# Finer orders at stage borders and in a mixer: weight splits, half-tile transposes, bank pairs, forget logits and last level scores

## The reference

```
x = layernorm(a*x + concat(retention(x@w_in), pool(x@w_in)) @ w_out)        # wout1, ln1
x = layernorm(a*x + (silu(conv3(gate)) * val) @ w_down)                    # up1, down1, ln2
x = x + 0.5*rms(swiglu(rms(x), ffn1_w_in, ffn1_w_down))                    # upA, downA
q_a,f_a,i_a,g_a,q_b,k_b,v_b,f_b,gates = rms(x) @ w_in_2                    # win2, 36 half blocks
o_a = rms(hgrn2(q_a,f_a,i_a)) * silu(g_a)   # scores with products of decays, in levels
o_b = softmax(q_b k_b^T + cumulated log sigmoid(f_b)) v_b                  # forgetting attention
x = x + rms((gate0*(o_a@w_a) + gate1*(o_b@w_b)) @ w_out_2)                 # brA, brB, wout2
x = x + rms(cross_attention(rms(x), rms(mem)) @ w_mo)                      # mq, mk, mv, mo
x = x + 0.5*rms(swiglu(rms(x), ffn2_w_in, ffn2_w_down))                    # upB, downB
```

## Time and profile before

| | us |
|---|---|
| median of 3 runs (1146.81 to 1151.43) | 1147.98 |
| profiled execution, device time | 1149.37 |
| its span | 1147.3 |
| PE busy | 1114.6 (97%) |
| PEld busy | 931.9 (81%) |
| DVE busy | 702.4 (61%) |
| ACT busy | 589.7 (51%) |
| DMA, mean over the span | 174 GB/s |

### The profile page before, as it was taken

The page is one execution under the profiler, slowest core; times in us unless marked ns, Lnnn a source line. Parts: engine busy times, 40 slices in busy tenths (PEclk is TensorE's granted clock), DMA queues, the critical chain, the costliest instruction groups (busy, mean ns, idle before and its releaser), DMA issues.

```text
span 1147.3 us, 13384 instructions
## 1 busy us (share of the span) xinstructions
PE 1114.6 (97%) x5370; PEld 931.9 (81%) x5370; DVE 702.4 (61%) x806; ACT 589.7 (51%) x777; POOL 41.7 (4%) x49
## 2 busy tenths in 40 slices
PE   7999999999999999999999999999999989999998
PEld 5887888888788888888888888888888767888886
DVE  4548566665776555566976765657547355765541
ACT  4463655554374634466545535536355456655441
POOL 1900000000000000000000000010000000000000
PEclk9999999999999999999999999999999999999999
DMA  9654655555575555475343443356555324656540
GB/s 370 212 182 143 216 177 172 183 181 185 176 244 183 184 183 183 147 257 172 123 147 116 142 147 127 130 211 230 177 177 202 124 74 146 197 182 195 183 162 37
DMA packets 125901, 200.14 MB, mean 174 GB/s; under 512 B 6288, under 2 KB 74048, under 8 KB 125712
## 3 DMA queue, kind: packets, MB, share of 16 engines
q1 hardware_dynamic: 122624, 187.78, 48.8%
q0 software_dynamic: 3216, 11.51, 2.8%
HBM read 198.22 MB, written 1.05 MB: 174 GB/s over the span
## 4 chain that ended last, share of the span: by engine, by line
PE 87%; DVE 7%; ACT 3%; issue 2%; DMA 1%; DVEq 0%; SPq 0%; ACTq 0%
PE ps L573 22%; PE ps L575 22%; PE ps L574 21%; PE ps L714 4%; PE ps L610 3%; PE ps L612 3%; PE ps L611 3%; PE ps L889 2%; DVE rest L1576 2%; ACT high L1101 1%; PE ps L1019 1%; PE ps L1032 1%; DVE rest L1581 0%; PE ps L675 0%; PE ps L677 0%
## 5 line engine op out<-in xcount | busy, mean ns | idle before, releaser
L1576 DVE TENSOR_TENSOR rest<-raw,high 128x2048 fp32r<-128x2048 f32 (+1 forms) x136 | 306.1, 2279 | 140.7 <-ACT high L1101 140.7
L573 PE MATMUL ps<-high,xt_high 128*128 128x512 f32 x896 | 356.5, 398 | 3.7 <-DVE rest L1576 2.1
L575 PE MATMUL ps<-high,xt_rest 128*128 128x512 f32 x896 | 350.6, 391 | 0.0
L574 PE MATMUL ps<-rest,xt_high 128*128 128x512 f32 x896 | 350.0, 391 | 0.0
L1101 ACT ACTIVATE high<-raw 128x2048 fp32r<-128x2048 f32 (+1 forms) x133 | 248.6, 1902 | 37.4 <-DMA raw<-in_ffn_w_down_dram 22.5
L573 PEld LDWEIGHTS ps<-high,xt_high 128*128 128x128 f32 x896 | 169.1, 189 | 37.4 <-issue 2.5
L575 PEld LDWEIGHTS ps<-high,xt_rest 128*128 128x128 f32 x896 | 168.9, 188 | 36.1
L574 PEld LDWEIGHTS ps<-rest,xt_high 128*128 128x128 f32 x896 | 169.2, 189 | 33.4
L1581 DVE SCALAR_TENSOR_TENSOR rest<-raw,wgain,high 128x512 fp32r<-128x512 f32 x176 | 119.0, 746 | 46.6 <-ACT high L1105 46.6
L1105 ACT ACTIVATE high<-raw,wgain 128x512 fp32r<-128x512 f32 x176 | 110.9, 721 | 9.5 <-DMA raw<-in_ffn_w_in_dram 9.5
L1323 ACT ACTIVATE act<-ps,recips 128x256 f32<-128x256 f32 x44 | 18.5, 471 | 98.6 <-PE ps L575 98.6
(11 more groups left out here) (320 smaller groups left out, 1313.9 us busy)
## 6 DMA issues: line engine op xcount, KB each, us to landing
raw<-in_w_in_dram SPq DMA_DIRECT2D x92, 512.0 KB, 4.2
raw<-in_ffn_w_in_dram SPq DMA_DIRECT2D x88, 512.0 KB, 4.7
raw<-in_w_up_dram SPq DMA_DIRECT2D x44, 512.0 KB, 4.6
raw<-in_ffn_w_down_dram SPq DMA_DIRECT2D x44, 512.0 KB, 4.1
raw<-in_w_down_dram SPq DMA_DIRECT2D x22, 512.0 KB, 4.3
raw<-in_w_out_dram SPq DMA_DIRECT2D x16, 512.0 KB, 4.5
raw<-in_w_mkv_dram SPq DMA_DIRECT2D x16, 512.0 KB, 4.6
raw<-in_w_branch_a_dram SPq DMA_DIRECT2D x8, 512.0 KB, 4.2
```

The lines of the kernel that those rows point to most:

```text
L573: pe.matmul(out, sh, wh, start=first, stop=False)
L574: pe.matmul(out, sh, wr, start=False, stop=False)
L575: mm = pe.matmul(out, sr, wh, start=False, stop=last)
L1576: vec.tensor_tensor(rest[:, slot, c], raw[:, slot, c], high[:, slot, c].bitcast(F32), ALU.subtract).then_inc(sem("lead_rest") if lead else ...
```

## The change

1. `wout1` begins with pair 1 instead of pair 0 (its weights are loaded in that order), and pair 0 comes next. For `mo` the new table gives the order that it had.
2. At the borders of `ln1` and `ln2`, DVE splits two units of the next stage before the statistics of tile 0 instead of three, and the third between the statistics of the two column halves.
3. At all four borders, transposes are ordered by column half. Only half 0 of tile 0 is transposed before the last products of tile 1, half 1 behind them; in `first_units` half 0 of tile 1 stands before unit 2 of tile 0, half 1 behind it.
4. `post_norm` on ACT puts the addition of the offset to the first partial sum (L1182) ahead of the second square instead of behind it.
5. In the mixer DVE does the subtraction of the forget logits at the head of u = 5 and the scan and memsets at the head of u = 7, each before that step's weight split.
6. The scores of level 128 are computed between the two halves of the half block u = 16 and 25, and only the outputs behind it.

```
+HALF_ORDER = {"wout1": ((1, 1), (0, 1), (0, 0), (1, 0)), "mo": ((0, 0), (1, 0), (0, 1), (1, 1))}
...
-                    for n, half in enumerate(HALVES[name]):
-                        for j in range(2):
-                            load_block((u + 2 * n + j,), w, j * NB, (half,))
+                    for n, (j, half) in enumerate(HALF_ORDER[name]):
+                        load_block((u + n,), w, j * NB, (half,))
...
-            def unit(u, products, wait=None):
+            def unit(u, products, between=None):
...
+                    if between and n == len(products) // 2:
+                        between()
...
-            def tile_transposes(key, src, ready, tt):
-                for q in range(2):
+            def tile_transposes(key, src, ready, tt, parts=(0, 1)):
+                for q in parts:
                     ready(tt, q)
                     transposes((key, 2 * tt + q), [src(tt, 4 * q + c) for c in range(4)])
...
+                    if n == 0:
+                        tile_transposes(key, src, ready, tt, (1,))
                     if n < 2:
                         wait_taken((key, 2 * tt + n))
                     elif tt == 0:
-                        tile_transposes(key, src, ready, 1)
+                        tile_transposes(key, src, ready, 1, (0,))
...
-            alternate("wout1", 0)
+            alternate("wout1", 1, 0)
...
-                    tile_transposes("x1", from_x, x1_ready, 0)
-
-            by_tiles(UNIT["wout1"] + 1, lambda tt: [(k, chunk_products("wout1", (1, 0, 1)[k], int(k > 0), tt),
+                    tile_transposes("x1", from_x, x1_ready, 0, (0,))
+
+            by_tiles(UNIT["wout1"] + 1, lambda tt: [(k, chunk_products("wout1", (0, 0, 1)[k], int(k > 0), tt),
...
-                if lv == 128:
-                    wait_taken(*(("lv", hf, v, g) for v in (0, *LEVELS, 128) for g in range(1 if v else 2)))
...
+            def level_outputs(hf):
+                wait_taken(*(("lv", hf, v, g) for v in (0, *LEVELS, 128) for g in range(1 if v else 2)))
...
+                last_levels = [n for n in HG_SLOT[u] if HG_STEPS[n][1] == 128]
                 if u >= LEAD:
-                    half_block("win2", j, half)
+                    half_block("win2", j, half, between=(lambda: levels(last_levels[0])) if last_levels else None)
...
                 square_half(tt, 0, name)
                 if between:
                     split_to(between)
+                act.wait_ge(sem("squared"), squared[0])
+                part_offset(tt)
                 square_half(tt, 1, name)
-                act.wait_ge(sem("squared"), squared[0] - 1)
-                part_offset(tt)
                 settle()
...
                 for n in range(2):
+                    if n == 1 and between:
+                        split_to(between)
...
-            split_to(UNIT["up1"] + LEAD)
-            layer_stats("wout1", 0)
+            split_to(UNIT["up1"] + 2)
+            layer_stats("wout1", 0, UNIT["up1"] + LEAD)
...
-            split_to(UNIT["upA"] + LEAD)
-            layer_stats("down1", 0)
+            split_to(UNIT["upA"] + 2)
+            layer_stats("down1", 0, UNIT["upA"] + LEAD)
...
+                if u == 5:
+                    vec.wait_ge(sem("flog_ln"), 1)
+                    vec.tensor_tensor(flog[:, :, :], flabs[:, :, :], flmin[:, :, :], ALU.subtract).then_inc(sem("flog_ready"), 1)
+                if u == 7:
...
                 split_to(UNIT["win2"] + u + 5)
```

More of the change, by code:

```diff
@@ L590, in wait_pair, with half_block @@
                     pe.wait_ge(pair_taken[n], used)
-            def half_block(name, j, half, th=xt_high, tr=xt_rest):
+            def half_block(name, j, half, th=xt_high, tr=xt_rest, between=None):
                 if half == 0:
@@ L595, in half_block @@
                 tiles = [chunk_products(name, j, half, tt, th, tr) for tt in range(TT)]
-                unit(UNIT[name] + 2 * j + half, [tiles[tt][k] for k in range(4) for tt in range(TT)])
+                unit(UNIT[name] + 2 * j + half, [tiles[tt][k] for k in range(4) for tt in range(TT)], between)
             def by_tiles(u, passes, before=None):
@@ L793, in _ @@
                 transposes(("mixr", tt), [rout[:, tt, c * P:(c + 1) * P] for c in range(4)])
-            wait_pair("wout1", 1)
+            wait_pair("wout1", 0)
             def x1_ready(tt, q):
@@ L966, in _ @@
                 for n in HG_SLOT[u]:
-                    levels(n)
+                    if n in last_levels:
+                        level_outputs(HG_STEPS[n][0])
+                    else:
+                        levels(n)
                 if u in OA_SLOT:
@@ L1059, in _ @@
             wait_taken(("om", 0), ("om", 2))
-            alternate("mo", 0)
+            alternate("mo", 0, 0)
             mem_transposes(2)
             mem_transposes(3)
-            alternate("mo", 1)
+            alternate("mo", 1, 1)
             mem_outputs(2)
@@ L1067, in _ @@
             wait_taken(("om", 1), ("om", 3))
[L1068 removed]
+            last_halves("mo", lambda: tile_transposes("f2", from_x, f2_ready, 0, (0,)))
             ffn("upB", "downB", "hB", "f2", f2_ready)
@@ L1697, in attention_out, with layer_stats @@
                 took(key, vec.tensor_tensor(dst, src, sums_.unsqueeze(2).to_broadcast([P, TT, width]), ALU.mult))
-            def layer_stats(product, tt):
+            def layer_stats(product, tt, between=None):
                 for n in range(2):
+                    if n == 1 and between:
+                        split_to(between)
                     c = slice(n * NB, (n + 1) * NB)
@@ L1973, in _ @@
                         diff(n + 1)
+                if u == 5:
+                    vec.wait_ge(sem("flog_ln"), 1)
+                    vec.tensor_tensor(flog[:, :, :], flabs[:, :, :], flmin[:, :, :], ALU.subtract).then_inc(sem("flog_ready"), 1)
+                if u == 7:
+                    src = ps[0:HH, AUX["flog", 1][1], 0:S]
+                    aux(("flog", 1))
+                    took(("flog", 1), vec.tensor_tensor_scan(fcum[:, :], fones[:, :], src, 0.0, ALU.mult, ALU.add))
+                    vec.wait_ge(aux_taken[AUX["flog", 1][1]], AUX["flog", 1][2] + 1)
+                    step(vec.memset(fcum_high[:, :].bitcast(F32), 0.0))
+                    step(vec.memset(fcum_rest[:, :].bitcast(F32), 0.0))
+                    settle()
+                    vec.sem_inc(sem("fcum_ready"), 1)
                 split_to(UNIT["win2"] + u + 5)
```

43 lines of the change are left out of this document (15 added, 28 removed).

## The result

The changed kernel takes 1142.99 us (median of 20 runs, 1141.07 to 1147.51), the kernel before 1149.19 beside it (20 runs, 1144.95 to 1151.43): a ratio of 0.9952, 95% interval 0.9941 to 0.9963. It is 5.5 us faster by the ratio (4.3 to 6.8); the two medians lie 6.2 apart. Forecast were 1143.0, a gain of 4.3 to 5.8 on the 1147.98 of three runs. The profiled execution took 1146.17 with a span of 1144.1, 3.2 less than the one before. 1143.6 was forecast for it. So the median came out as forecast and the profiled execution did not, and TensorE's clock has a part in both. One run of the kernel before, 1411.81 us at a granted clock of 0.75, stands beside the first experiments and is left out of all that follows.

What follows compares the result with a forecast made beforehand. PE, busy 97% of the span, was taken as the bound, with only idle time to win. Terms 0 + 1.5 + 1.6 + 0 + 0.3 + 0.4 + 2.0 = 5.8 (4.3 without the fall) gave 1143.0 from 1147.98; range 1139.8 to 1146.4.

Steps and rivals of the forecast that it cites:

- `wout1`, edit 1: At wout1, PE's 1.16 idle before the first product goes, but the retention half waits 1.3 for `xt_rest`: gain 0, bounds 0 and 1.3.
- ln1, edits 2 and 3: Border of ln1: the 0.79 wait goes, 0.99 stays, tile 1 waits 1.2; gain 1.5, or 0 without a clock fall.
- ln2, edits 2 and 3: Border of ln2: waits of 0.72, 0.79 and 0.59 go, a new 1.15 comes; gain 1.6, bounds 0.9 and 2.6.
- m2: Border m2: no wait before; ACT and DVE take half 1 about 1.4 later, using spare time; gain 0, bounds -1.5 and 0.
- forget logits, edit 5: Waits of 1.20 and 0.86 go, PE waits about 1 for `hqk` at level 1; gain 0.4, bounds 0.2 and 2.4.
- f2, edit 3: At f2 the 2.06 wait behind DVE stays; moving half 1's transposes behind 12 matmuls gains 0.3.
- Splitting eight into two fours costs nothing by that: Price of transposes on PE: four take 0.44, eight 0.87, so ordering them by column half adds no time.
- it comes 0.3 to 0.4 earlier: Before the level 1 scores: DVE's work up to `hqk` changes only its order, comes 0.3 to 0.4 earlier, PE waits about 1.
- if only one wait is left there I expect no fall: At ln1: with one of the waits 0.99 and 0.79 left, the clock does not fall; the fall lost 1.6 us.
- the clock gives nothing: Rival: the fall comes elsewhere or is not due to these waits; 4.3 in the profiled execution, 1144.5 from the median; chance 0.26, shared with longer new waits.
- All waits simply go: Rival: each touched PE wait vanishes, 12.4 in sum, giving 1137 or 1136; chance of more than 6.5 gained 0.15.
- slower: Rival: x half 0 of tile 1 comes late at all four borders, with clock falls; 6.0 slower, 1154; chance 0.04.

Runs made afterwards that it cites:

- the last version: Changed kernel with statistics of tile 1 first at ln1 and ln2, plus three DVE weight splits moved later: 1139.07 us, ratio 0.9912 to the kernel before.

## Why the prediction was right, and where it was not

**By its own steps**, what the traces show without falls of the clock:

| step | forecast | measured |
|---|---|---|
| `wout1`, edit 1 | 0 | 0 |
| ln1, edits 2 and 3 | 1.5 with the fall, 0 without | 1.5 (15.34 less 13.88) with, -0.1 without |
| ln2, edits 2 and 3 | 1.6 | 1.5 |
| m2 | 0 (-1.5 to 0) | -0.2, of which 0.1 is the shift between the columns |
| forget logits, edit 5 | 0.4 (0.2 to 2.4) | 0.2 |
| level 128, edit 6 | 2.0 | 2.1 |
| f2, edit 3 | 0.3 | 0.1 |
| edit 4 | 0 (-0.1 to 0.3) | 0 |
| sum | 5.8, or 4.3 without the fall | 5.2, or 3.6 |

The sum has a check of its own. From x1 half 0 to the last matmul the kernel before takes 1036.64 us with two falls, the changed one 1034.60 with three; with 1.58 taken off for each fall, 3.6 is between them.

The mechanisms of the waits held at every place. At `wout1` the step "It will come 1.3 earlier, at 91.2, and wait 1.3 there" is the 1.45 at 91.33. At ln1 and ln2 the new waits were put at 1.2 and 1.15 and are 0.95 and 0.97 as idle time (1.1 from start to start), and x of tile 1 is ready when forecast. At level 128 the forecast was 0.95 + 1.1, and the copy behind the split no longer stops PE. One price was wrong, "Splitting eight into two fours costs nothing by that": at f2 the 0.3 is there at the first product behind half 1 of tile 0, but only 0.1 of it is left at the last matmul, and ln1 and m2 each lose about 0.1 by their order.

**Edit 5 was mis-sized** by 0.2. The step that was off is "it comes 0.3 to 0.4 earlier": `hqk` ends at 554.60 (the row at 553.91), against 558.64 before. That is 4.04 earlier where PE was already 4.08 ahead at `upA`, so edit 5 only made up the 0.2 of the row m2. In edit 5 alone the stretch shrinks by 0.2 (244.41 against 244.62). That DVE's chain was the limit, and the wait at level 1 its new place, was forecast rightly, and so was the transpose of `stage` as what is late next (0.80 of idle; in edit 5 alone it starts 228.62 after `upA` tile 1, before 229.00, so the 0.4 of the forecast is right there). Half of it is gone by `hqk`; where, isn't shown.

**The account of the profiled execution.** Of 5.2 with the fall at ln1, plus 1.2 at the head, less two later falls of 1.6 more than before had, 3.2 is left, and 3.2 is measured. The forecast of 1143.6 had the orders nearly right and knew nothing of the last two terms.

**The clock was the weak step.** The forecast had "most of this 1.5 is the clock", and that is right of the execution compared: 15.34 in that stretch against 13.76 without a fall. But it went on to "if only one wait is left there I expect no fall" as if the edit took it away. The waits of rows 4 had a fall behind them in one of seven executions. By that, as an estimate, the edit saves 0.2 there on the mean, and it costs 0.1 by its order.

The Trainium skill's page TensorE: Matmul & The Clock Gate, section "HAM oscillation — how this bites in real kernels", has the clock fall behind gaps several times as long as 0.99 and 0.79. It is borne out to this extent, that these two mostly brought none; but the pair 0.90 and 1.62 at the second `mo` border brought one in 13 of 14 executions and the 1.11 before level 1 in one of the five that have it. Each wait is shorter than what the page speaks of. The measurement decides: here falls came right behind waits of 1 to 2 us, at one place nearly always, at others now and then. A rival reading is open. Between 0.90 and 1.62 stand only eight transposes, so that PE is 3.6 us without a product of 128x512 there (930.81 less 0.90 to 933.50), as long as the page's gaps, against 2.9 at ln1. But the same 3.6 at the first `mo` border had a fall in eight of fourteen, so the length alone doesn't decide either.

**The median.** The ratio's 5.5 (4.3 to 6.8) is more than the 3.6 that the orders give. Time multiplied by clock is 4.1 less in the 20 runs of after than in the 74 of before, near those 3.6. The mean clock is 0.9968 against 0.9957, worth another 1.2. Four of the 20 runs are at 0.995 or less, 35 of the 74. This is the rest of the gain, as far as the record shows it: the runs of before that the ratio was taken from have no clocks on record, and the 74 stand in other sets. Nor is it shown that the change brings fewer falls. With edit 5 undone the clock is 0.9958 against 0.9955 of before beside it. The profiled executions have two falls in each of three of before and three late ones in each of two of after, and these two (1146.17 and 1147.48) are slower than most runs of their kernel. The steps within the runs are not all falls either: seven runs of after stand at 1141.1 to 1142.1 and eight at 1142.8 to 1143.2, all at 0.997 or 0.998. The slow start that the clock column can miss would fit that; it isn't shown.

So the agreement of 1142.99 with 1143.0 is luck in two parts. The forecast added up 4.3 to 5.8 where the orders gave 3.6, and the clock brought about 1.2 more. And it started from 1147.98, the median of three runs, where 20 have 1149.19: with the 5.0 that it took off it would have said 1144.2. The rival "the clock gives nothing" (4.3 in the profiled execution) was nearer to what the orders gave, and the profiled execution's 3.2 is even below it, by two later falls. "All waits simply go" fell with the new waits at four places, "slower" with the missing wait at m2.

## What to carry to other kernels

Follow what a moved step queues behind. Half 1's transposes behind 12 matmuls held DVE for 2.51 and so the whole norm of the next tile; an order that lets DVE do the next tile's statistics in that time was worth 2.3 us more, and moving the splits themselves behind what PE waits for 3.6 more, together 5.9, more than the change itself. When a change of some microseconds is to be judged, subtract the starts of the same instruction in two traces, stretch by stretch, and set aside stretches with a fall of the clock: that told some 0.1 us here, where the ratio of two sets of 12 runs of one kernel differed by 2.2 us. Where every run's mean clock is on record, multiply the time with it before comparing: that told the versions apart within 0.9 us. And look at the clock itself: edits 5 and 6 alone each won time by their order and had a lower clock in about half of their runs.

## What the runs showed of the hardware

- A fall of the granted clock to half costs 1.5 to 1.6 us each time (15.34 against 13.76, 127.41 against 125.78), for 9 or 10 matmuls in 3.4 us instead of 16 to 18. At one place it stood behind the same waits in one execution and not in the next.
- The pace at the start varies too: the first products stood 0.43 us apart for over 5 us in one execution of the kernel before and 0.23 from the second on in another. The first retention product stood between 89.58 and 92.62 us after the span's start over thirteen executions, all but that of the last version, which moves it; edit 1, the only other change ahead of it, leaves it where it was.
- With both together, executions of one kernel (edit 6 alone) took from 1141.2 to 1149.8 us. Why a fall comes in one execution and not in another is open. How low the clock is on the mean does depend on the kernel: 17 of the 36 runs of edits 5 and 6 alone had 0.993 or less, one of 74 of the kernel before and none of 20 of the changed one. What in the order brings that is open as well.
